# An mLSTM block's running maxima: from selector matmuls to a broadcast load and an addition on GpSimd

## What is computed

```python
causal = jnp.tril(jnp.ones((CHUNK, CHUNK), dtype=bool))
d_log = jnp.where(causal, b[..., :, None] - b[..., None, :] + ig[..., None, :], -jnp.inf)
m_t = jnp.maximum(b + m_prev[..., None], jnp.max(d_log, axis=-1))
w_intra = jnp.exp(d_log - m_t[..., None])
scores = jnp.einsum('bhcld,bhcsd->bhcls', q, k) * w_intra
```

## Time and profile before

| | us |
|---|---|
| median of 3 runs | 1812.57 |
| lowest and highest of them | 1809.74, 1814.12 |
| span of the profiled execution | 1808.6 |
| TensorE busy in it | 1761.9 |
| VectorE, ScalarE, GpSimd busy | 1119.1, 991.3, 680.6 |

### The profile page before, as it was taken

The page is one execution under the profiler, slowest core; times in us unless marked ns, Lnnn a source line. Parts: engine busy times, 40 slices in busy tenths (PEclk is TensorE's granted clock), DMA queues, the critical chain, the costliest instruction groups (busy, mean ns, idle before and its releaser), DMA issues. The chain is left out here.

```text
span 1808.6 us, 28177 instructions
## 1 busy us (share of the span) xinstructions
PE 1761.9 (97%) x8972; PEld 1437.3 (79%) x8972; DVE 1119.1 (62%) x1776; ACT 991.3 (55%) x2041; POOL 680.6 (38%) x942
## 2 busy tenths in 40 slices
PE   7999999999899999999999999998999999999998
PEld 6888888878577887888878887886788888788887
DVE  5431214555479898979797979894666666533333
ACT  5431213322277787878787878784677776411111
POOL 1100000000147777777777777772234444200000
PEclk9999999999999999999999999999999999999999
DMA  6677766121394647454656453735555454422220
GB/s 199 163 192 215 232 186 186 52 87 47 126 282 131 172 144 212 135 175 135 174 171 185 135 176 127 249 118 190 169 193 159 162 189 139 162 77 79 81 82 40
DMA packets 193733, 277.05 MB, mean 153 GB/s; under 512 B 66684, under 2 KB 128380, under 8 KB 184408
## 3 DMA queue, kind: packets, MB, share of 16 engines
q1 hardware_dynamic: 190952, 265.19, 47.8%
q0 software_dynamic: 2672, 10.52, 1.7%
HBM read 187.41 MB, written 88.26 MB: 152 GB/s over the span
## 5 line engine op out<-in xcount | busy, mean ns | idle before, releaser
L975 PE MATMUL b_late<-w_split,spare 128*128 128x512 f32 x1416 | 411.4, 415 | 2.5 <-ACT b_p_out L1057 2.3
L756 POOL TENSOR_TENSOR b_a_lo<-b_aT,b_a_hi 128x512 fp32r<-128x512 f32 (+2 forms) x312 | 354.8, 1137 | 25.0
L1138 DVE TENSOR_TENSOR_SCAN b_buf<-b_y,b_buf 128x511 f32<-128x511 f32 (+2 forms) x320 | 357.9, 1118 | 9.1
L529 PE MATMUL a_po<-uT_hi,w_split 128*128 128x512 f32 x1024 | 318.6, 392 | 2.3 <-DVE w_split L397 2.3
L975 PEld LDWEIGHTS b_late<-w_split,spare 128*128 128x128 f32 x1416 | 243.4, 190 | 40.5 <-issue 4.6
L752 POOL CAST b_a_hi<-b_aT 128x512 fp32r<-128x512 f32 (+1 forms) x320 | 182.1, 569 | 179.1 <-PE b_o L949 147.6
L1148 DVE SCALAR_TENSOR_TENSOR b_buf<-b_buf,b_y 128x512 f32<-128x512 f32 (+2 forms) x320 | 187.9, 587 | 70.0 <-PE b_y L935 69.0
L529 PEld LDWEIGHTS a_po<-uT_hi,w_split 128*128 128x128 f32 x1024 | 193.0, 188 | 46.4 <-DVE w_split L397 2.7
L1034 ACT ACTIVATE b_aT<-b_turned 128x512 f32<-128x512 f32 (+1 forms) x320 | 170.3, 532 | 67.6 <-POOL b_a_lo L756 60.1
L529 PE MATMUL a_po<-uT_lo,w_split 128*128 128x512 f32 x512 | 201.6, 394 | 0.0
L1043 ACT ACTIVATE b_buf<-b_y 128x512 f32<-128x512 f32 (+2 forms) x320 | 171.3, 535 | 50.1 <-PE b_y L929 47.7
(11 more groups left out here) (244 smaller groups left out, 3359.6 us busy)
## 6 DMA issues: line engine op xcount, KB each, us to landing
spare<-u_pair SPq DMA_DIRECT2D x62, 1024.0 KB, 5.4
proj_n<-b_p_out SPq DMA_DIRECT2D x59, 256.0 KB, 5.7
c_gates<-proj_n SPq DMA_DIRECT2D x16, 768.0 KB, 4.5
w_raw<-in_w_in POOLq DMA_DIRECT2D x5, 2048.0 KB, 10.1
x_in<-in_x SPq DMA_DIRECT2D x16, 512.0 KB, 3.9
qk_hi<-stage_hi SPq DMA_DIRECT2D x32, 256.0 KB, 2.6
qk_lo<-stage_lo SPq DMA_DIRECT2D x32, 256.0 KB, 2.9
u_pair<-uT_hi SPq DMA_DIRECT2D x16, 512.0 KB, 3.7
```

The costliest lines, as they stand in the source:

```text
L529: mm = pe.matmul(po[t][:], w[:, k, m * P:(m + 1) * P], u[:, k, t * GROUP:(t + 1) * GROUP], start=(k == 0 and n == 0), stop=(k == KT - 1 an ...
L756: nc.gpsimd.tensor_tensor(lo[:, cols], raw, hi[:, cols].bitcast(F32), ALU.subtract).then_inc(lo_done, 1)
L975: mm = pe.matmul(late[:], u_in[f % US][:, u_part, k, :], w[:, k, :], start=(i == 0), stop=(i == PASSES - 1))
L1138: nc.vector.tensor_tensor_scan(down, y[u % YS][:, 1:keys][:, ::-1], down, b[:, keys - 1:keys], ALU.add, ALU.subtract).then_inc(log_done, 1)
```

## The change

The maxima are kept in f32, in four rows of 2048 (`neg_m_rows`). Each tile's 4 x 128 values are loaded into all 128 partitions by one DMA that reads them 128 times (`neg_m`, two buffers of 128 x 4 x 128 f32, 256 KB each). Tiles 0 and 1 are loaded in the attention stage, tile c + 1 at the end of SyncE's step c. GpSimd adds the triangle `hidden` to the buffer one tile ahead (`hide_future`), and ScalarE takes its exponential from there. The matmuls L1641 and L1643, the three bf16 parts and the selector are gone. VectorE, no longer behind ScalarE's wait for the scores, waits for them itself. The last two tiles are taken out of the loop and written out, since the last has no next tile to load. `c_gap` keeps the addresses behind it where they were.

```diff
@@ mlstm_constants (GpSimd) @@
-                for t in (ml.ident, g.m_before, ml.ident_b, ml.hidden, ml.sel, ml.state):
+                for t in (ml.ident, g.m_before, ml.state):
...
+                nc.gpsimd.memset(ml.hidden[:], 0.0).then_inc(g.zeroed, 1)
+                pool.wait_ge(g.zeroed, 4)
                 nc.gpsimd.affine_select(out=ml.hidden[:], in_=ml.hidden[:], compare_op=ALU.is_ge, fill=MASKED, base=0,
-                                        pattern=[[0, 2], [1, P]], channel_multiplier=-1).then_inc(g.consts_ready, 1)
-                for part in range(M_PARTS):
-                    if part:
-                        pool.wait_ge(g.sel_ready, part)
-                    nc.gpsimd.affine_select(out=ml.sel[:], in_=ml.sel[:], compare_op=ALU.not_equal, fill=1.0,
-                                            base=-part * H, pattern=[[-1, H], [0, P]], channel_multiplier=1)\
-                        .then_inc(g.sel_ready, 1)
+                                        pattern=[[1, P]], channel_multiplier=-1).then_inc(g.consts_ready, 1)
@@ attention stage, SyncE @@
-                    sp.wait_ge(g.parts, 5)
-                    sp.dma_start(neg_m_rows.rearrange("a r t -> r a t"), ml.neg_m_parts[:]).then_inc(ml.neg_m_stored, 16)
+                    sp.wait_ge(g.dve, 13)
+                    sp.dma_start(neg_m_rows.rearrange("h (c t) -> (h c) t", t=P), ml.neg_m_row[:]).then_inc(ml.neg_m_stored, 16)
                     other_loads(sp)
@@ attention stage, VectorE @@
-                if n in (41, 42, 43):
-                    part = n - 41
...
-                    nc.vector.tensor_copy(ml.neg_m_parts[:, part, :], ml.neg_m_row[:]).then_inc(g.parts, 1)
-                    if part < M_PARTS - 1:
-                        dve.wait_ge(g.parts, 2 * part + 1)
-                        nc.vector.tensor_tensor(ml.neg_m_row[:], ml.neg_m_row[:], ml.neg_m_parts[:, part, :],
-                                                ALU.subtract).then_inc(g.parts, 1)
@@ MlstmBuffers @@
-        self.ident_b = sb("c_ident_b", [P, P], BF16)
-        self.hidden = sb("c_hidden", [P, 2, P], BF16)
-        self.sel = sb("c_sel", [M_PARTS * H, H, P], BF16)
         self.neg_m_row = sb("c_neg_m_row", [H * TOK, P])
-        self.neg_m_parts = sb("c_neg_m_parts", [H * TOK, M_PARTS, P], BF16)
-        self.neg_m = sb("c_neg_m", [M_PARTS * H, SEQ], BF16)
+        self.neg_m = sb("c_neg_m", [P, 2, H, P])
+        self.hidden = sb("c_hidden", [P, P])
+        sb("c_gap", [P, 2048 // 4])
@@ mlstm_and_output_projection @@
-        scores = psum("c_scores", [P, 2, 2, P])
+        scores = psum("c_scores", [P, 2, P])
...
-            with fori(0, (TOK - FIRST) // 2) as n:
+            with fori(0, (TOK - FIRST) // 2 - 1) as n:
                 for s in range(2):
                     step(2 * n + (FIRST + s), s)
-            for c in range(TOK, TOK + LAG):
+            for c in range(TOK - 2, TOK + LAG):
                 step(c, c % 2)
@@ SyncE, at the end of step(c, s) @@
+                if has_next(c) and not (isinstance(c, int) and c == 0):
+                    until(sp, weights_done, 2 * c)
+                    sp.dma_start(neg_m[:, 1 - s], neg_m_rows[:, tile(c + 1)].unsqueeze(0).broadcast_to([P, H, P]))\
+                        .then_inc(ml.neg_m_loaded[1 - s], 16)
@@ TensorE, score(c, s, p) @@
-                if isinstance(c, int) and (c, p) == (0, 0):
-                    pe.wait_ge(ml.neg_m_loaded, 16)
                 until(pe, p_done, u)
                 for i in range(2):
-                    pe.matmul(scores[:, 0, i, :], k[:, i, :], q[:, i, :], start=True, stop=True)
-                pe.matmul(scores[:, 1, :, :], ident_b[:], hidden[:], start=True, stop=False)
-                for i in range(2):
-                    mm = pe.matmul(scores[:, 1, i, :], sel[:, 2 * p + i, :], neg_m[:, tile(c)],
-                                   start=False, stop=(i == 1))
+                    mm = pe.matmul(scores[:, i, :], k[:, i, :], q[:, i, :], start=True, stop=True)
                 mm.then_inc(scores_done, 1)
@@ ScalarE, weigh @@
-                until(act, scores_done, u + 1)
+                until(act, neg_m_masked, c + 1)
                 until(act, intra_done, u - 1)
                 for i in range(2):
-                    a = nc.scalar.activation(wt[p][:, i, :], scores[:, 1, i, :], ACT.Exp,
+                    a = nc.scalar.activation(wt[p][:, i, :], neg_m[:, s, 2 * p + i, :], ACT.Exp,
                                              bias=cols[:, A, 2 * p + i, at(c)])
@@ GpSimd @@
+            def hide_future(c, s):
+                pool.wait_ge(ml.neg_m_loaded[s], loads(c, s, 16))
+                nc.gpsimd.tensor_tensor(neg_m[:, s], neg_m[:, s], hidden[:].unsqueeze(1).broadcast_to([P, H, P]),
+                                        ALU.add).then_inc(neg_m_masked, 1)
...
             def step(c, s):
                 if has(c, NORM_LAG):
                     head_norms(c - NORM_LAG, (s - NORM_LAG) % 2)
+                if has_next(c):
+                    hide_future(c + 1, 1 - s)
                 if has(c, LAG):
                     post_norm(c - LAG)
                     add_residual(c - LAG, (s - LAG) % 2)
+            hide_future(0, 0)
             steps(pool.Fori, step)
@@ VectorE @@
             def weights_times_scores(c, p):
+                until(dve, scores_done, 2 * c + p + 1)
                 until(dve, weights_done, 2 * c + p + 1)
-                nc.vector.scalar_tensor_tensor(out=wt[p][:], in0=scores[:, 0, :, :], scalar=ML_SCALE, in1=wt[p][:],
+                nc.vector.scalar_tensor_tensor(out=wt[p][:], in0=scores[:], scalar=ML_SCALE, in1=wt[p][:],
@@ other_loads @@
-            sp.dma_start(ml.neg_m[:], neg_m_rows.rearrange("a (h c) t -> (a h) (c t)", h=ML_HEADS))\
-                .then_inc(ml.neg_m_loaded, 16)
+            for n in range(2):
+                sp.dma_start(ml.neg_m[:, n], neg_m_rows[:, n * P:(n + 1) * P].unsqueeze(0).broadcast_to([P, ML_HEADS, P]))\
+                    .then_inc(ml.neg_m_loaded[n], 16)
```

More of the change, by code:

```diff
@@ L758, in mlstm_constants @@
             def mlstm_constants():
-                for t in (ml.ident, g.m_before, ml.ident_b, ml.hidden, ml.sel, ml.state):
+                for t in (ml.ident, g.m_before, ml.state):
                     nc.gpsimd.memset(t[:], 0.0).then_inc(g.zeroed, 1)
                 nc.gpsimd.memset(g.one[:], 1.0).then_inc(g.consts_ready, 1)
[L762 to L765, removed]
-                nc.gpsimd.affine_select(out=ml.hidden[:], in_=ml.hidden[:], compare_op=ALU.is_ge, fill=MASKED, base=0,
-                                        pattern=[[0, 2], [1, P]], channel_multiplier=-1).then_inc(g.consts_ready, 1)
-                for part in range(M_PARTS):
-                    if part:
-                        pool.wait_ge(g.sel_ready, part)
-                    nc.gpsimd.affine_select(out=ml.sel[:], in_=ml.sel[:], compare_op=ALU.not_equal, fill=1.0,
-                                            base=-part * H, pattern=[[-1, H], [0, P]], channel_multiplier=1)\
-                        .then_inc(g.sel_ready, 1)
+                pool.wait_ge(g.zeroed, 3)
+                nc.gpsimd.affine_select(out=ml.ident[:], in_=ml.ident[:], compare_op=ALU.not_equal, fill=1.0, base=0,
+                                        pattern=[[-1, P]], channel_multiplier=1).then_inc(g.consts_ready, 1)
+                nc.gpsimd.memset(ml.hidden[:], 0.0).then_inc(g.zeroed, 1)
+                pool.wait_ge(g.zeroed, 4)
+                nc.gpsimd.affine_select(out=ml.hidden[:], in_=ml.hidden[:], compare_op=ALU.is_ge, fill=MASKED, base=0,
+                                        pattern=[[1, P]], channel_multiplier=-1).then_inc(g.consts_ready, 1)
                 nc.gpsimd.memset(ml.minus_half[:], -0.5).then_inc(g.consts_ready, 1)
@@ L1327, in __init__ @@
         self.eps = sb("c_eps", [P, SB_HEADS + H])
-        self.ident_b = sb("c_ident_b", [P, P], BF16)
-        self.hidden = sb("c_hidden", [P, 2, P], BF16)
-        self.sel = sb("c_sel", [M_PARTS * H, H, P], BF16)
         self.neg_m_row = sb("c_neg_m_row", [H * TOK, P])
-        self.neg_m_parts = sb("c_neg_m_parts", [H * TOK, M_PARTS, P], BF16)
-        self.neg_m = sb("c_neg_m", [M_PARTS * H, SEQ], BF16)
+        self.neg_m = sb("c_neg_m", [P, 2, H, P])
+        self.hidden = sb("c_hidden", [P, P])
+        sb("c_gap", [P, 2048 // 4])
         self.neg_m_stored = ctx.enter_context(nc.semaphore("neg_m_stored"))
-        self.neg_m_loaded = ctx.enter_context(nc.semaphore("neg_m_loaded"))
+        self.neg_m_loaded = [ctx.enter_context(nc.semaphore(f"neg_m_loaded{n}")) for n in range(2)]
         self.cols = sb("c_cols", [P, 4, H, TOK])
@@ L1408, in __init__ @@
         self.consts_ready = sem("c_consts_ready")
-        self.sel_ready = sem("c_sel_ready")
-        self.parts = sem("g_parts")
 def mlstm_and_output_projection(nc, ml, x, w_hi, w_lo, w_tiles, w_raw, post_norm_w, ml_t, proj_n, y_rows,
```

(14 more changed lines are left out.)

8 lines of the change are left out of this document (1 added, 7 removed).

## The result

The changed kernel takes **1828.39 us** (median of four runs, 1827.0 to 1830.1), against 1811.5 for the kernel before in the same measurement (1809.74 to 1814.12, four runs). The ratio is 1.0093 with a 95% interval of 1.008 to 1.0105: slower by 0.9%, 16.9 us. The forecast was 1798.2 us and a gain of 14.4. The profiled execution of the changed kernel has a span of 1828.3 us.

What follows compares the result with a forecast made beforehand. TensorE, busy 1761.9 of the 1808.6 us span, was taken as the bound. Gains of 14.9 - 0.5 = 14.4 us, other parts zero, gave a span of 1794.2, plus 4.0 to the median: 1798.2 us, range 1794.5 to 1805.

Steps and rivals of the forecast that it cites:

- Part 1: TensorE, mLSTM and output projection stage: the mask matmuls leave its queue in 32 units, saving 14.9 us.
- part 2: Output projection, fourth tile: TensorE's wait for VectorE's last weight split grows from 2.3 to 2.8 us, hiding 0.5 us.
- the reading by starts: TensorE's mask matmuls priced by differences of matmul starts, 0.42 us a unit and 0.67 in the first: 13.7 us.
- that by the weight loads: TensorE's mask matmuls priced by starts of weight loads, 0.53 us a unit: 17.3 us with the cold first unit, upper bound.
- "issue" idleness: Rival, TensorE: the 0.21 us idle before L1643 would stand before L1648 instead; gain 6.3 us, 1806.3 us; chance 0.07.
- lower bound: TensorE's mask matmuls, supposing L1648 has its own price for waiting on the kw buffer: 0.35 us a unit, 11.2 us.
- Part 3: GpSimd's sixteen triangle additions, 1.33 us each, fit its idle time; holding up VectorE costs nothing, at worst 0.17 us.
- Part 4: SyncE's extra 256 KB load a tile: 1.5 us at most, q and k land in 6.2 of 7.3 us; cost zero.
- third rival: Load, GpSimd's addition, residual sum, store and next load form a loop, 18.0 us a tile: 1819 us; chance 0.05.
- first rival: SyncE's q and k load lands later than 7.3 us; at 9.3 it loses 11 us, 1809.4 us; chance 0.09.
- another engine: Rival: an engine other than TensorE takes over, half or nothing of the gain, 1805 to 1812.6 us; chance 0.05.

Runs made afterwards that it cites:

- e4_no_load: Changed kernel without the third stage's broadcast loads of the maxima, except those of the first two tiles, whose masked maxima serve all tiles; 1797.47 us, ratio 0.9925.
- f2_pitch: Changed kernel with the rows of the maxima 8.5 KB apart in memory instead of 8 KB; 1796.42 us, ratio 0.9921.
- g3_pitch12k: Changed kernel with the rows of the maxima 12 KB apart instead of 8 KB; 1799.07 us in a single run.
- e1_early: Changed kernel with the maxima's load issued earlier, behind the load of x and ahead of SyncE's wait for the store; 1798.59 us, ratio 0.9924.
- g2_late: Changed kernel with the maxima's load issued behind the loads of q, k and v of its own tile instead of ahead; 1831.06 us.

## Why the prediction was wrong

**Part 1, right.** The undisturbed tile takes 16.12 us; 16.1 was forecast. The turning of k starts 0.44 behind the scores, or 0.45, with nothing between (1383.07 and 1383.52 above). The gain without the slow load is 13.6 us (e4_no_load) and 14.1 (f2_pitch, 1810.47 - 1796.42). Less the 0.5 of part 2, the reading by starts was 13.2 and that by the weight loads 16.8: the runs lie near the starts, and within their intervals, some 4 us either way, they don't tell 13.2 from the 14.4 of the sum. That some of the "issue" idleness would stay did not come true. A slip in the lower bound changes nothing: 0.42 - 0.06 is 0.36 us a unit, 11.5 us, not 11.2.

**Part 2, right.** The wait for the last split grew from 2.3 us to 2.7, 2.8 in others; 2.8 was forecast.

**Part 3, right for its own price.** The additions take 1.26 to 1.48 us, with medians of 1.28 to 1.35. In the kernel with the rows 8.5 KB apart one of them follows the gating at once and GpSimd still has time left (order of time, GpSimd, answering):

```profile
1363.65 1.34 POOL L1860 TENSOR_TENSOR c_y<-c_y,c_gates 128x512 f32<-128x512 f32 x1 [1.90 <-DVE c_y L1928]
1364.94 1.35 POOL L1866 TENSOR_TENSOR c_neg_m<-c_neg_m,c_hidden 128x512 f32<-128x512 f32 x1
1368.00 0.20 POOL L1872 TENSOR_TENSOR c_post_rstd<-c_post_ss 128x1 f32<-128x1 f32 x1 [1.70 <-ACT c_junk L1803]
```

It holds VectorE up a second time, as was reckoned. The group of the four products, before and then with the 8.5 KB (1330 to 1500 us; busy us, mean ns):

```profile
L1943 DVE SCALAR_TENSOR_TENSOR c_y<-c_num,c_rstd,c_gates 128x128 f32<-128x128 f32 x40 | 21.7, 602 | 0.0
```

```profile
L1934 DVE SCALAR_TENSOR_TENSOR c_y<-c_num,c_rstd,c_gates 128x128 f32<-128x128 f32 x44 | 34.4, 840 | 0.0
```

That is 4 x 0.24 = 0.95 us a tile, and TensorE has no wait from it.

**Part 4, the step that failed.** "By the 768 KB of the gates in 4.4 us, 256 KB are 1.5 us at most" priced the new transfer by its bytes, from rows in which every partition reads its own address. It measured 10.1 us to landing, and it holds up what is queued behind it: q and k took 11.4, not 6.2. All else in this part held. The limit was put at 7.3 us from issue to landing: with 7.5 (g3_pitch12k) TensorE begins to wait, 2.9 us in 3 times, and with 6.3 it doesn't (the one wait of e1_early, whose median is 5.9, is for a load that took 14.5). The price was put at (L - 7.3)/2 a tile for 11 tiles: at 11.4 it is 22.6 us, and the waits are 23.3. They come as 3.5 to 4.3 us in every second tile; the halving is thus right in size, but its reason, loads that run two tiles ahead, is not shown by any run. What this formula left out is the clock. TensorE's busy time in the changed kernel is 1757.6 us against this, with the same 8876 matmuls at 8.5 KB (page, part 1):

```profile
PE 1749.9 (97%) x8876; PEld 1434.5 (80%) x8876; DVE 1128.7 (63%) x1771; ACT 992.9 (55%) x2041; POOL 698.3 (39%) x952
```

23.3 of waits and 1757.6 - 1749.9 = 7.7 of matmuls that run longer make 31.0; the two spans differ by 1828.3 - 1797.2 = 31.1. Nearly all of the longer matmuls lie in the third stage: up to 1250 us TensorE's busy time differs by 0.6 us between the two. So a third as much again as the stalls goes to the clock that falls in them.

The evidence was on the table. The prediction itself quoted the one broadcast load among other transfers, 10.8 us, and used it in the third rival for the maxima's own loop; it didn't use it in part 4 and in the first rival, where q and k stand in the queue behind the same load. There the slowest landing of the old kernel, 9.3, was taken for the worst case. Had the bound of the one place been carried to the other, 10.8 and more for q and k would have given (10.8 - 7.3)/2 x 11 = 19 us of loss, 1817.5 us by the prediction's own limit: a slower kernel, by 4.9 us, just inside the 5.4 that it held to be noise. The 7.7 of the clock, which no term of the prediction has, would still have been missing. That row proved near in size; whether its 10.8 has the same cause was not tried.

**The rivals.** The first, q and k late, is what happened, beyond the 9.3 that it was priced at (11 us on 1798.2 is 1809.2, where it says 1809.4). No rival reached 1828: the worst was 1819, and slower had 0.06. The third, the loop, is real and its formula good to 0.2 us in g2_late, but at the 10.1 us of the changed kernel it is the shorter of the two, 17.4 us a tile against 18.7. Issue idleness and another engine did not show.

**From span to median.** The 4.0 us that lay between the profiled span and the median before are no constant of the kernel: here it is 0.1, and at 8.5 KB the median lies 0.8 under the span. Between the time and the span of one and the same execution it is 1.8 us in every run (1830.1 and 1828.3 here); the rest is scatter between executions.

## What to carry to other kernels

Price a transfer by a row of the same kind of addressing, not of the same bytes, and give that price to everything queued behind it too: a bound that is used in one rival belongs in every step that the same instruction touches. Where a DMA sends a few short rows from memory to all partitions, look at the distance of those rows: here 8 KB was slow and 12 KB in between, and next to each other or padded by a piece's length they were fast. And a stall on TensorE that came again every second tile cost a third more than its own length, for the clock fell in it.

## What the runs showed of the hardware

Reading the same 512 bytes, or four rows of 512 bytes 8 KB apart, for 512 pieces takes 10 us from issue to landing; at 12 KB it takes 6.5 and at 8.5 KB 4.9. Not only that transfer is held: while it is on its way the 16 DMA engines are busy and move little. The loads of q, k and v stand right behind it. The first 6 us of such a stretch in the changed kernel (load issued at 1343.39), then the same stretch with the rows 8.5 KB apart (load issued at 1343.60), in the columns of the earlier trace rows:

```profile
1345.00:1351.00 6.00, 6.00 (x39) 5.33 (x38) 2.83 (x7) 5.18 (x12) 1.29 (x2) 1.00 0.86 63
```

```profile
1345.00:1351.00 6.00, 6.00 (x30) 4.92 (x29) 5.32 (x10) 5.69 (x9) 3.43 (x3) 1.00 0.73 197
```

The engines are busy for 0.86 of the time at 63 GB/s, against 0.73 at 197. In the 8 us after it the changed kernel catches up, at 289 GB/s. Where on the way the pieces queue up, in the memory or ahead of it, none of these runs can show.
